# Expert weights asked for in another order: a two-layer GLA, convolution, attention and MoE step on one Trainium2 core

## The reference, cut to what matters

```python
act = jax.nn.silu(jnp.einsum('td,edf->tef', t, w_gate)) * jnp.einsum('td,edf->tef', t, w_up)
routed = jnp.einsum('tef,efd->td', act * gate[:, :, None], w_down)
shared = (jax.nn.silu(t @ sh_gate) * (t @ sh_up)) @ sh_down
```

## Time and profile before

| | us |
|---|---|
| median of 3 runs | 1458.87 |
| profiled execution | 1457.95 |
| its span in the profile | 1455.9 |
| TensorE busy | 1372.9 (94%) |
| VectorE busy | 375.2 (26%) |
| ScalarE busy | 259.7 (18%) |
| HBM read | 495.15 MB |

### The profile page before, as it was taken

One profiled execution on the slowest core, in us unless ns is written; L12 is line 12 of the kernel. 1 busy time (PEld: TensorE's weight loads), 2 busy tenths in 40 slices (PEclk: granted clock), 3 DMA queues, 4 the chain that ended last, 5 costly groups with the idle time before them and its releaser, 6 DMA issues.

```text
span 1455.9 us, 27256 instructions
## 1 busy us (share of the span) xinstructions
PE 1372.9 (94%) x11756; PEld 708.3 (49%) x11757; DVE 375.2 (26%) x1056; ACT 259.7 (18%) x493; POOL 108.3 (7%) x355
## 2 busy tenths in 40 slices
PE   4999999999999999999789998999999999999996
PEld 4676756444344444344256665644443444434442
DVE  3291456011111111011036526431111111111112
ACT  1414215111011111111023331331110111101110
POOL 7300800000000000000000034000000000000000
PEclk9999999999999999999899999999999999999998
DMA  9665965999999999999964773659999999999995
GB/s 354 212 233 202 387 237 202 351 366 422 421 420 393 415 421 421 420 420 395 393 221 155 276 259 129 266 206 353 395 421 420 420 393 411 420 421 420 392 411 236
DMA packets 110456, 499.08 MB, mean 343 GB/s; under 512 B 14960, under 2 KB 20988, under 8 KB 60924
## 3 DMA queue, kind: packets, MB, share of 16 engines
q1 hardware_dynamic: 109820, 496.19, 85.6%
q0 software_dynamic: 384, 1.05, 0.2%
q10 hardware_dynamic: 128, 0.03, 0.0%
HBM read 495.15 MB, written 2.10 MB: 342 GB/s over the span
## 4 chain that ended last, share of the span: by engine, by line
PE 81%; DMA 8%; DVE 5%; ACT 3%; issue 2%; SPq 1%; DVEq 0%; ACTq 0%
PE ps L1068 25%; PE ps L1087 11%; PE ps L1094 10%; PE ps L1054 8%; PE ps L760 5%; PE ps L757 4%; PE ps L938 4%; DMA store<-in_exp_w_up 4%; DMA ring<-in_exp_w_up 3%; PE ps L368 3%; PE ps L868 2%; DVE ring L1649 2%; PE ps L704 1%; PE ps L1114 1%; DMA ring<-in_w_ada 1%
## 5 line engine op out<-in xcount | busy, mean ns | idle before, releaser
L1068 PE MATMUL ps<-ring,h 128*32 128x512 f32 x2592 | 363.6, 606 | 26.7 <-DMA store<-in_exp_w_up 16.4
L1068 PEld LDWEIGHTS ps<-ring,h 128*32 128x32 f32 x2592 | 105.1, 112 | 221.9 <-issue 221.9
L1068 PE MATMUL ps<-store,h 128*32 128x512 f32 x736 | 190.7, 609 | 6.2 <-issue 6.2
L1087 PE MATMUL ps<-ring,work 128*32 128x512 f32 x1296 | 191.5, 598 | 1.5 <-ACT work L1452 1.5
L1094 PE MATMUL ps<-store,work 128*128 128x512 f32 x400 | 185.0, 605 | 0.0
L1054 PEld LDWEIGHTS ps<-tm,work 128*128 128x128 bf16 x2496 | 144.4, 98 | 44.3 <-issue 43.1
L1054 PE MATMUL ps<-tm,work 128*128 128x128 bf16 x2496 | 156.9, 219 | 0.3
L1094 PEld LDWEIGHTS ps<-store,work 128*128 128x128 f32 x400 | 71.9, 189 | 113.7 <-issue 113.7
L1824 DVE TENSOR_TENSOR work<-work,ps 128x256 f32<-128x256 f32 x52 | 21.9, 422 | 396.8 <-ACT work L1448 396.8
L1826 DVE COPY store<-ps 128x512 f32<-128x512 f32 x52 | 36.0, 692 | 340.8 <-PE ps L1087 340.8
L1448 ACT ACTIVATE work<-ps 128x256 f32<-128x256 f32 x52 | 20.0, 384 | 467.9 <-PE ps L1068 467.9
(11 more groups left out here) (316 smaller groups left out, 1146.9 us busy)
## 6 DMA issues: line engine op xcount, KB each, us to landing
ring<-in_exp_w_gate SPq DMA_DIRECT2D x102, 1024.0 KB, 11.7
ring<-in_exp_w_up SPq DMA_DIRECT2D x102, 1024.0 KB, 13.9
ring<-in_exp_w_down SPq DMA_DIRECT2D x102, 1024.0 KB, 14.0
ring<-in_w_ada SPq DMA_DIRECT2D x24, 2048.0 KB, 12.1
store<-in_exp_w_gate SPq DMA_DIRECT2D x26, 1024.0 KB, 11.8
store<-in_exp_w_up SPq DMA_DIRECT2D x26, 1024.0 KB, 14.4
work<-in_exp_w_down SPq DMA_DIRECT2D x26, 1024.0 KB, 12.8
ring<-in_w_in SPq DMA_DIRECT2D x6, 2048.0 KB, 12.4
```

The source lines that it names most:

```text
L1068: last = mm(ps[first:first + TILE, 4, :], X_e[:, b, kt, first:first + TILE], gate_up(slot, kt), start=(kt == 0), stop=(kt == KT - 1))
L1087: last = mm(ps[first:first + TILE, y_bank, :], turn[:, P * j + first:P * j + first + TILE], down(slot, j, half), start=(j == 0), stop=(j = ...
```

## The change

Each chosen expert's gate and up request is a "G" and its down request a "D". A fixed string of 61 G and 61 D now gives the order; G and D are each in the order of the experts. The waits stay: each G waits by `gate_free`, each D by `down_free`. A D now reads the expert's number again. Line numbers shift by 4 from L140 on.

```diff
+GATE_UP_THEN_DOWN = ("GDGGGDDDGGDDGGGDDGDGDDGGGGDDDDGGDGDGDDGGDDGGDDGGDDGGGDGDDGDD"
+                     "GGDGDDGGDDGGDDGGGDGDDDGGDGDGDDGGDDGGDDGGDDGGGDGDDGDGDGDGGGDD"
...
-                for p in range(PASSES):
-                    wave = [k for k in range(EARLY, EXPERTS) if EXPERT_PASS[k] == p]
-                    e = {}
-                    for k in wave:
-                        r = LOADED[k][1]
-                        e[k] = sp.value_load(order_i[0:1, r:r + 1], min_val=0, max_val=EXPERTS - 1)
-                        load_in(k, [A[w][layer, bass.ds(e[k], 1)][0] for w in ("exp_w_gate", "exp_w_up")])
-                    for k in wave:
-                        down_free(k)
-                        load_down(sp, expert_slot(k), A["exp_w_down"][layer, bass.ds(e[k], 1)][0],
-                                  down_in[expert_slot(k)])
+                def chosen_expert(k):
+                    r = LOADED[k][1]
+                    return sp.value_load(order_i[0:1, r:r + 1], min_val=0, max_val=EXPERTS - 1)
+
+                k_in = k_down = EARLY
+                for kind in GATE_UP_THEN_DOWN:
+                    if kind == "G":
+                        e = chosen_expert(k_in)
+                        load_in(k_in, [A[w][layer, bass.ds(e, 1)][0] for w in ("exp_w_gate", "exp_w_up")])
+                        k_in += 1
+                    else:
+                        assert k_down < k_in
+                        e = chosen_expert(k_down)
+                        down_free(k_down)
+                        load_down(sp, expert_slot(k_down), A["exp_w_down"][layer, bass.ds(e, 1)][0],
+                                  down_in[expert_slot(k_down)])
+                        k_down += 1
```

More of the change, by code:

```diff
@@ L139 @@
 assert sorted(r for p, r in LOADED) == list(range(EXPERTS)) and all(sum(ws) == P // TILE for ws in WIDTHS)
+GATE_UP_THEN_DOWN = ("GDGGGDDDGGDDGGGDDGDGDDGGGGDDDDGGDGDGDDGGDDGGDDGGDDGGGDGDDGDD"
+                     "GGDGDDGGDDGGDDGGGDGDDDGGDGDGDDGGDDGGDDGGDDGGGDGDDGDGDGDGGGDD"
+                     "DD")
+assert len(GATE_UP_THEN_DOWN) == 2 * (EXPERTS - EARLY) and GATE_UP_THEN_DOWN.count("G") == EXPERTS - EARLY
 LEFT_ROUNDS = 2
```

## The result

The changed kernel takes 1448.45 us in the median of 5 runs (1444.39 to 1449.52), the one before 1459.10 (1457.92 to 1460.99) beside it. The medians lie 10.7 us apart, and the ratio is 0.9917, 95% interval 0.9898 to 0.9935: about 0.8% faster, inside the range, 4.5 us above the forecast.

The account below looks back on a forecast made before the run. The prediction took the weight-copy queue to bound the expert stage, its idle moments being lost for good. From 1457.95 us it took 16.1 for filled gaps and added 2.0, giving 1443.9, so 1444 us, range 1438 to 1454.

Parts of the forecast that it names:

- The queue is the bound over the stage, and its dry moments are lost for good: Expert stage: weight copies need 18.4 us a pass against TensorE's 17.45, so idle queue time is never recovered.
- The sum of the gaps: Four low-rate stretches a layer, by four-expert passes: missing time 7.8 us in layer 0 and 8.4 in layer 1.
- The term of 16.1 us: Both layers' last passes start earlier by the queue's missing time once no gap is left: minus 16.1 us in total.
- pass 25 of layer 0 starting near 711 instead of 718.25: Sign of being right: layer 0's last pass starts near 711, still after a 5 to 7 us wait on up weights.
- The levelling: Levelling lost, taken as 2.0 us added back in the forecast sum over both layers.
- Rival A: Slowest of 16 DMA engines sets the pace, so half the saving, 7.5 us, remains: 1450.4 us; chance 0.16.
- SP's work: Each down request's extra number read and address, 0.75 us, hidden by waits or queue: taken as 0, at most 6 us.
- New waits: Passes 4 and 13 start about 1 and 2 us late, then slower clock: some 5 us a layer, not added.
- the cover for the new waits: Last pass's wait for the queue, 7.6 us before and still 5 to 7, absorbs the delays at earlier passes.
- B: Rival: no change, as new queue gaps open elsewhere while TensorE frees slots every 17.45 us; 1457 us; chance 0.08.
- C: Rival: slower, as down copies go ahead of gate and up copies a pass waits on; 1467 us; chance 0.07.
- D: Rival: all weight waits and the slow clock go in both layers, 42 us saved; 1416 us; chance 0.03.

Follow-up runs that it names:

- E3: Changed kernel's list with only next-pass gate and up copies moved ahead, no down copies ahead of a four-expert pass's last gate and up; 1454.31 us, 0.9979 of the kernel before.
- E5: Changed kernel plus one swap a layer: at pass 17 a second down copy ahead of the fourth expert's gate and up; 1450.35 us, 0.9955 of the kernel before.
- E6: Changed kernel with one pass 23 expert's three copies cut to an eighth of their bytes (probe, weights left out); 1444.29 us, 0.9912 of the kernel before.
- E8: Changed kernel with the three copies of pass 25's first expert cut to an eighth of their bytes (probe); 1440.47 us, 0.9879 of the kernel before.
- E10: Changed kernel with four-expert passes moved to 2, 9, 13, 19, 23, 25, one-expert pass at 24, list refitted; 1442.33 us, 0.9888 of the kernel before.
- E12: Repeat, beside the unaltered changed kernel, of the version with four-expert passes at 2, 9, 13, 19, 23, 25; 1441.48 us, 0.9885 of the kernel before.
- E2: Changed kernel's list with only down copies moved ahead at four-expert passes, next-pass gate and up copies left behind; 1464.62 us, 1.0040 of the kernel before.
- E9: Changed kernel with the old request order restored at passes 12 to 14; 1448.84 us, 0.9945 of the kernel before.
- E11: Changed kernel run again unaltered, for comparison with the spread four-expert passes; 1448.58 us, 0.9934 of the kernel before.
- E1: Changed kernel with the old list, keeping each down request's second reading of the expert number; 1457.83 us, 1.0001 of the kernel before.
- E4: Changed kernel with the new list around passes 4 to 8 only, the old one from pass 12 on; 1452.49 us, 0.9952 of the kernel before.
- E7: Changed kernel with four-expert passes moved to 2, 8, 12, 18, 22, 25, list refitted; 1445.97 us, 0.9930 of the kernel before.

## Why the prediction was right, and where

*What bounds the kernel.* "The queue is the bound over the stage, and its dry moments are lost for good" is the step that failed. E3 leaves the first gap open and gains 3.3 and 3.6 us; E5 fills a gap and gains nothing, with pass 17 1.9 and 2.0 us late; E6 takes 6.5 us of copies away, lets the queue idle at 327 GB/s and gains 0.4 and 0.8. What bounds is, by turns, TensorE (passes 8 to 10 and 19 to 21 keep 17.45 us in both kernels) and, around each four-expert pass, the chain slot free, request, copies queued behind it, landing, pass. For the last pass it can be read off the changed kernel: SP asks for the next gate copy at 675.16, just after pass 23's gate and up products,

```profile
675.16 0.34 SPq L398 DMA_DIRECT2D ring<-in_exp_w_gate  x1
```

and the twelfth copy from there, the up weights that pass 25 waits for, lands at 693.17 + 16.8 = 710.0:

```profile
693.17 16.83 DMA store<-in_exp_w_up
710.25 8.64 PE ps L1078 x64
```

From 675.16 to the start at 710.25 it is 35.1 us; TensorE's own work from the same moment takes 27.9; the difference is the wait of 7.1. E8 shortens that chain and the wait shrinks, E6 shortens what lies ahead of it by more and less comes of it, and with three copies fewer in the chain (E10, E12) the wait is gone. That this chain bounds the last pass is shown; for the other four-expert passes it is inferred from E2, E5 and E9, where a late landing or a late pass is seen at passes 17 and 18 and no bytes were taken out.

*The sum of the gaps* still gave nearly the right size. From the start of pass 3 to that of pass 25 the changed kernel took 398.33 us in layer 0 and 398.19 in layer 1:

```profile
311.92:710.25 398.33, 386.61 (x3437) 169.02 (x3430) 55.55 (x122) 47.15 (x88) 0.00 (x0) 0.99 1.01 418
1018.46:1416.65 398.19, 386.61 (x3437) 168.99 (x3429) 55.54 (x122) 47.15 (x88) 0.00 (x0) 0.99 1.01 419
```

398.33 x 418 is 166.5 MB. Before it was 403.9 us for the same copies:

```profile
314.37:718.25 403.88, 388.66 (x3437) 169.89 (x3430) 55.57 (x122) 47.19 (x88) 0.00 (x0) 0.98 1.00 412
```

Bytes over time is the mean rate whatever the cause, so any change that raises the mean rate between two fixed points of the same list shortens the stretch; the gaps measured the loss and did not cause it. The forecast was safe as long as the mean rate rose as assumed, and that it did was luck in part. E2 shows how near the other case was: half of the same edits, aimed at the same gaps, has a ratio of 1.0040.

*Its size.* The term of 16.1 us came out as 12.2 in the first profile (5.55 and 6.60 between these points), and 13.1 with the last passes; E11 has 11.0 for the two stages. Part of what is missing is the gap that opened at 545 to 560 us, 15 x (1 - 391/421) = 1.1 us, and 0.9 us for the one in layer 1; in E11 also the longer last wait of layer 0. The sign "pass 25 of layer 0 starting near 711 instead of 718.25" was met by 710.25, but 2.5 us of these 8.0 come from a stage that began earlier (256.1 against 258.6; in E11, with the same list, it began at 258.7); counted from pass 3 it is 5.55.

*The levelling* of 1.0 us a layer cannot be told from these rates. At 418 GB/s the stretch of layer 0 lacks 398.33 x (1 - 418/421) = 2.8 us, of which the new gap explains 1.1; before, at 412 GB/s, it lacks about 8.6, of which the four gaps explain 7.8. That leaves 1.7 against 0.8, a difference of the size of the term, but half a GB/s of rounding is already 0.5 us. No run separates it. Rival A, half the gain, is the number nearest to the median (1450.4 against 1448.45); its sign, a last pass only 3 to 4 us earlier, did not appear (5.55 and 6.60 us).

*SP's work* at nothing: right, by E1.

*New waits.* Pass 4 was to start 1 us late and did (18.73 instead of 17.45 us for pass 3). Pass 13 was to wait 2 us and then run at the lower clock: it waited 2.1 us, and its gate and up part took 8.77. The 6.87 us that the prediction sets against 8.77 and 9.40 is a row that begins 0.2 us after its pass; the whole part takes 7.05, so the slow clock costs 1.7 us and not 1.9. Not forecast: pass 12 starts 1.1 us late, and pass 23, one of those that were to have no wait, 0.7. The wait before pass 25 was to stay at 5 to 7 and was 7.1 and 8.4, so the cover for the new waits held.

*Rivals.* B (gaps open elsewhere) happened once a layer, at passes 16 and 17, for about 1 us. C is what E2 turned out to be, and by its mechanism: the four-expert passes start late behind the down copies ahead of them, and the queue runs dry elsewhere. What C did not have is why it runs dry, the gate copies held back behind a waiting down copy. D did not happen; even in E12 some 12 us of weight waits a layer are left.

*Open.* The stage of layer 0 begins at 256.1 us in the first profile of the changed kernel and at 258.7 in E11, and the part between the stages takes 235.3 and 233.4 us. Neither lies in what was changed. But the part between the stages took 232.5 us in both profiles with the old order (the kernel before and E1) and 233.0 to 235.3 in all twelve others, so some of what the stages gain may be lost there; no run here separates the causes. How the slow part of the clock after a wait depends on the wait was not tried; 7.1, 7.6 and 8.4 us of wait were followed by 8.64, 9.40 and 9.63 us, but 4.5 us by 9.79 and 8.3 us (E4) by 8.60.

## What to carry to other kernels

Idle time of a queue is a symptom. Before adding it up, ask of each gap what the next waiting instruction was short of: if it is a slot, filling the gap or taking bytes away helps little, and putting copies into it can delay the one that is needed. In an in-order request list, moving one request earlier pays only if what then stands in front of the next urgent request does not wait longer; test the halves of such an edit apart, since one of them can be a loss. When demand comes in bursts (here four experts in one pass), try spreading the bursts as well as ordering the requests inside them: the order gave 0.7 to 0.8%, the second spread a further 0.5%. Where they are put matters, since the first spread (E7) is not clear of the changed kernel.

## What the runs showed that was not expected

A short wait of TensorE can cost twice. In the changed kernel pass 13 waits 2.1 us, and then the granted clock is 0.81 of full, a mixture of 2.4 and 1.2 GHz, during its gate and up part, which takes 8.77 us instead of 7.05. The 2.1 us of wait cost 3.8; waits of 1.1 us had no such cost (7.07 us).

```profile
491.03:499.80 8.77, 8.77 (x65) 2.88 (x65) 0.00 (x0) 0.00 (x0) 0.00 (x0) 0.81 1.01 419
```

But the length of the wait alone does not decide it. In layer 1 of E3 pass 18 waits 3.1 us, the longest "issue" wait of that stage, and then runs at full clock:

```profile
PE ps L1078 <- issue: 5.0, 2, 3.1
1293.92:1301.00 7.08, 7.08 (x65) 2.43 (x65) 0.00 (x0) 0.00 (x0) 0.00 (x0) 1.00 1.01 419
```

So did passes 17 and 18 of layer 1 in E1 after 2.0 us each. What else decides was not tried.

In E12 the waits of a layer are nearly as long in sum as in E11 (12.8 against 14.7 us in layer 0), but split into pieces, and the last pass runs at full clock. The mean granted clock of the run was 0.989, against 0.981 in E11.
